# Low one-hots of a PEER gate scatter made by ScalarE, one token at a time

## The reference

```python
q = (x_blk @ w_query).reshape(b, t, PEER_HEADS, 2, HALF_KEY)
scores = jnp.einsum('bthcd,hcnd->bthcn', q, sub_keys)
top_s, top_i = lax.top_k(scores, PEER_TOPK)
...
gate = jax.nn.softmax(best_s, axis=-1)
u = expert_u[expert_idx]
v = expert_v[expert_idx]
act = jax.nn.gelu(jnp.einsum('btd,bthkd->bthk', x_blk, u), approximate=False)
return jnp.einsum('bthk,bthkd->btd', (gate * act), v)
```

## Time and profile before

| | |
|---|---|
| median of 3 runs | 1572.77 us (1571.89 to 1572.81) |
| the profiled execution | 1576.24 us, span 1574.4 us |
| mean granted TensorE clock | 0.928 of full |
| expert scores without gates | about 770 to 977 us |
| gates beside expert scores | 977.7 to 1208.9 us |
| expert values | 1215.2 to 1568.6 us |

### The profile page before, as it was taken

One profiled execution on the slowest core, in us unless ns is written; L12 is line 12 of the kernel. 1 busy time (PEld: TensorE's weight loads), 2 busy tenths in 40 slices (PEclk: granted clock), 3 DMA queues, 4 the chain that ended last, 5 costly groups with the idle time before them and its releaser, 6 DMA issues.

```text
span 1574.4 us, 22797 instructions
## 1 busy us (share of the span) xinstructions
PE 1443.9 (92%) x8952; PEld 1253.7 (80%) x8952; DVE 884.4 (56%) x1571; ACT 745.4 (47%) x1356; POOL 908.5 (58%) x665
## 2 busy tenths in 40 slices
PE   5898998999998599979999989998998999999998
PEld 2685667689886598658999889988998888888886
DVE  4645884356411677543489955999997334322222
ACT  2442212455544466434444445444544555555554
POOL 0540001466765454135679998776776777767775
PEclk9895555999999799989999999999999999999999
DMA  9342342344555132114544545544555666555552
GB/s 387 124 161 107 107 161 107 114 182 163 184 187 187 61 128 108 54 58 149 195 163 163 184 161 182 180 168 168 175 180 204 229 244 249 219 187 189 195 195 90
DMA packets 48298, 261.65 MB, mean 166 GB/s; under 512 B 5440, under 2 KB 14016, under 8 KB 19008
## 3 DMA queue, kind: packets, MB, share of 16 engines
q1 hardware_dynamic: 37984, 249.58, 44.0%
q10 hardware_dynamic: 10208, 10.63, 1.9%
HBM read 250.75 MB, written 9.44 MB: 165 GB/s over the span
## 4 chain that ended last, share of the span: by engine, by line
PE 60%; DVE 24%; PEld 6%; POOL 3%; ACT 3%; issue 2%; DMA 1%; PEldq 1%; DVEq 0%; SPq 0%; ACTq 0%
PE bank L1297 22%; PE bank L699 18%; PE bank L731 17%; PEld bank L731 6%; DVE hotg L2454 5%; DVE hot L2451 4%; DVE hot L2450 4%; POOL v_lo L1782 3%; PE bank L1076 1%; DVE arena L2466 1%; DVE arena L1897 1%; DMA ring<-w_dram 1%; ACT arena L1353 1%; DVE ada L1897 1%; DVE arena L2334 1%
## 5 line engine op out<-in xcount | busy, mean ns | idle before, releaser
L1782 POOL TENSOR_TENSOR v_lo<-ring,v_hi 128x512 fp32r<-128x512 f32 x448 | 614.5, 1386 | 186.3 <-ACT v_hi L1712 176.7
L1774 POOL TENSOR_TENSOR v_lo<-ring,d_hi 128x512 fp32r<-128x512 f32 x213 | 293.7, 1388 | 468.8 <-ACT d_hi L1395 398.8
L1712 ACT CAST v_hi<-ring 128x512 fp32r<-128x512 f32 x512 | 317.3, 621 | 372.4 <-PE bank L699 211.2
L699 PE MATMUL bank<-hT_hi,v_hi 128*128 128x256 f32 x1024 | 294.7, 288 | 9.5 <-POOL v_lo L1782 9.5
L699 PE MATMUL bank<-hT_lo,v_hi 128*128 128x256 f32 x1024 | 289.6, 283 | 0.0
L699 PE MATMUL bank<-hT_hi,v_lo 128*128 128x256 f32 x1024 | 288.1, 281 | 0.0
L1395 ACT CAST d_hi<-ring 128x512 fp32r<-128x512 f32 x236 | 144.0, 620 | 184.9 <-PE bank L731 143.9
L1297 PE MATMUL bank<-v_hi,mix_hi 128*128 128x512 f32 x512 | 202.1, 395 | 3.2 <-DVE mix_lo L2481 3.2
L699 PEld LDWEIGHTS bank<-hT_hi,v_hi 128*128 128x128 f32 x1024 | 194.8, 190 | 11.1 <-POOL v_lo L1782 6.1
L1297 PE MATMUL bank<-v_hi,mix_lo 128*128 128x512 f32 x512 | 200.7, 392 | 0.0
L1297 PE MATMUL bank<-v_lo,mix_hi 128*128 128x512 f32 x512 | 199.2, 389 | 0.0
(11 more groups left out here) (316 smaller groups left out, 2413.0 us busy)
## 6 DMA issues: line engine op xcount, KB each, us to landing
ring<-w_dram SPq DMA_DIRECT2D x228, 1024.0 KB, 4.8
gate_dram<-gput ACTq DMA_DIRECT2D x64, 128.0 KB, 2.4
gget<-gate_dram SPq DMA_DIRECT2D x32, 256.0 KB, 4.9
x<-x_dram SPq DMA_DIRECT2D x1, 1024.0 KB, 5.6
arena<-mem_dram ACTq DMA_DIRECT2D x1, 1024.0 KB, 12.6
out_dram<-x SPq DMA_DIRECT2D x1, 1024.0 KB, 4.0
arena<-const_dram ACTq DMA_DIRECT2D x1, 884.0 KB, 8.7
arena<-vec_dram ACTq DMA_DIRECT2D x1, 144.0 KB, 4.6
```

The costliest lines, as they stand in the source:

```text
L699: return nc.tensor.matmul(out_, lhsT, rhs, start=start, stop=stop)
L1712: nc.scalar.copy(v_hi[:, r, :], quarter(at, r)).then_inc(s_vhi, 1)
L1774: nc.gpsimd.tensor_tensor(v_lo[:, r, :], dense_quarter(d, r), d_hi[:, r, :], ALU.subtract).then_inc(s_dpl, 1)
L1782: nc.gpsimd.tensor_tensor(v_lo[:, r, :], quarter(at, r), v_hi[:, r, :], ALU.subtract).then_inc(s_plo, 1)
```

## The change

`hotg` keeps only the products with the high part of the gates, made by VectorE as before in token pairs. The products with the low part are a new tile `hotl`, two buffers of 4 tokens x 128 keys, with the keys innermost. ScalarE makes it by four activations a group (`Copy` with a scale for each partition), one for each token, which read `hot2` with a step of four. The scale is the low part of the gate in fp32, which now overwrites `gateT`; it is no longer rounded to fp16 ahead of the multiplication. ScalarE does this behind the cast of quarter slot - 2 (and behind `second_gates`, if one stands there), and waits for `hot2` of the group.

```diff
-        hotg = sb("hotg", [2, 2, 2, P, 2], F16)
+        hotg = sb("hotg", [2, 2, P, 2], F16)
+        hotl = sb("hotl", [2, 4, P], F16)
...
                 pe.wait_ge(s_oh, e + 1)
+                pe.wait_ge(s_ohl, e + 1)
                 for i in range(4):
-                    for part in range(2):
-                        last = mm(ps[:, i * P:(i + 1) * P], hot1[:, e % 2, :, i], hotg[:, e % 2, part, i // 2, :, i % 2],
-                                  start=(part == 0), stop=(part == 1))
+                    cols = ps[:, i * P:(i + 1) * P]
+                    mm(cols, hot1[:, e % 2, :, i], hotg[:, e % 2, i // 2, :, i % 2], stop=False)
+                    last = mm(cols, hot1[:, e % 2, :, i], hotl[:, e % 2, i, :], start=False)
...
                     if g in COPY_TURN:
                         second_gates(COPY_TURN[g])
+                    if g + 2 in GATE_TURN:
+                        low_one_hots(GATE_TURN[g + 2])
+
+            def low_one_hots(e):
+
+                if e == 0:
+                    act.wait_ge(s_glo, 1)
+                act.wait_ge(s_eq, e + 1)
+                if e >= 2:
+                    act.wait_ge(s_gfull, e - 1)
+                for i in range(4):
+                    ins = nc.scalar.activation(hotl[:, e % 2, i, :], hot2[:, e % 2, :, i], ACT.Copy,
+                                               scale=gateT[:, 4 * e + i:4 * e + i + 1])
+                ins.then_inc(s_ohl, 1)
...
-            link(tt(gates[:, 1, :], gateT[:, :], gates[:, 0, :], ALU.subtract))
+            tt(gateT[:, :], gateT[:, :], gates[:, 0, :], ALU.subtract).then_inc(s_glo, 1)
...
                 if e >= 2:
                     dve.wait_ge(s_gfull, e - 1)
+                    dve.wait_ge(s_ohl, e - 1)
...
                 dve.wait_ge(s_eq, e + 1)
-                for part in range(2):
-                    ins = tt(hotg[:, b, part], hot2[:, b, :, :].rearrange("p n (a i) -> p a n i", a=2),
-                             gates[:, part, t:t + 4].rearrange("p (a i) -> p a i", a=2).unsqueeze(2).to_broadcast(
-                                 [P, 2, P, 2]), ALU.mult)
-                ins.then_inc(s_oh, 1)
+                tt(hotg[:, b], hot2[:, b, :, :].rearrange("p n (a i) -> p a n i", a=2),
+                   gates[:, 0, t:t + 4].rearrange("p (a i) -> p a i", a=2).unsqueeze(2).to_broadcast([P, 2, P, 2]),
+                   ALU.mult).then_inc(s_oh, 1)
```

More of the change, by code:

```diff
@@ L537, in build @@
         s_oh = sem("onehots_ready")
+        s_ohl = sem("low_onehots_ready")
+        s_glo = sem("low_gates_ready")
         s_gfull = sem("gate_tokens_full")
```

## The result

The changed kernel takes 1590.86 us (median of 4 runs, 1589.23 to 1591.80) against 1572.79: a ratio of 1.0114, 95% interval 1.0096 to 1.0131. It is slower, by 18 us. The forecast was slower by 51: the direction and the place were right, the size wasn't. The profiled execution took 1590.93 us, with a span of 1589.0 (before: 1574.4). The spans differ by 14.6 us and the medians by 18, because the execution profiled before was 3.5 us over its median; what follows goes by the spans.

A forecast was written before the change was run, and what follows sets the result against it. VectorE's throughput was taken to bound the gate stage. The longer lap through ScalarE's order cost 21 us and compares held by GpSimd 30: +51 us, 1624 us for the median, range 1582 to 1650.

The forecast's parts named there:

- What bounds the stage: Gate stage, first to last gate product: VectorE's throughput, slowed by GpSimd's subtractions, sets 3.66 us a lap (one token group).
- the loop: Per lap: hot2, low one-hots, cast, gate copy, gate product, first_gated, next hot2; 3.78 us, 4.0 with extras, 21 us lost.
- VectorE gets 0.33 us a lap back: One of two hotg products leaves VectorE: 20 us over 61 laps, not counted because the lap doesn't wait for it.
- ScalarE's own time: Four added activations a group take 1.2 us; ScalarE then has 3.2 of 3.66 us a lap, so its throughput suffices.
- ScalarE's place: Low one-hots wait for hot2 ahead of the gate copy in ScalarE's order, closing a 4.0 us lap: 21 us lost.
- the way from the end of the copy to TensorE: Semaphore delay between ScalarE's gate copy and TensorE's gate product, taken as 0.14 us from the wait for VectorE.
- a second cast: In 10 of 61 laps a further ScalarE cast of 0.52 us stands in the lap: 0.09 us a lap on average.
- What is late next: GpSimd's subtraction leads VectorE's compare by 0.08 us; lost races cost 1.06 us each, two thirds of 47 laps: 30 us.
- the case I had put at 1635 to 1656: Rival: GpSimd goes ahead of VectorE's compare throughout the gate stage, 1635 to 1656 us; chance 0.17.
- VectorE wins the race: Rival: VectorE's compare goes ahead of GpSimd's subtraction, leaving only the 21 us loss, 1594 us (1580 to 1605); chance 0.26.
- The hidden wait: Rival: ScalarE has room and its wait for hot2 hides; the kernel gets 20 us faster, 1553 us; chance 0.08.
- TensorE's granted clock: Rival: new gaps in the gate stage leave TensorE busy about 72% and lower its clock; no cost taken, no chance given.

The follow-up runs named there:

- the control with the earlier copy: Kernel before the change, with ScalarE's gate copy (second_gates) one quarter earlier: 1568.49 us, ratio 0.9981.
- later: Changed kernel with ScalarE's low one-hots (the hotl activations) one quarter later, at slot - 1: 1562.99 us, ratio 0.9926.
- earlier: Changed kernel with ScalarE's low one-hots one quarter earlier, at slot - 3, in 47 of 64 groups: 1640.79 us, ratio 1.0423.
- Gelu out: Changed kernel with the Gelu put ahead of the low one-hots where these follow a tile's last cast: 1581.73 us, ratio 1.0061.
- copy out: Changed kernel with the gate copy (second_gates) one quarter earlier, at slot + 4, low one-hots unmoved: 1572.91 us, ratio 1.0005.
- the parts alone: Kernel before the change plus only four ScalarE activations without the wait: 1574.31 us; plus only the wait for hot2: 1575.55 us.
- both: Kernel before the change plus the wait for hot2 and four activations on it, written to unread tiles: 1606.55 us, ratio 1.0223.
- the two runs with memsets: Changed kernel with one, or four, 128x1 VectorE memsets ahead of the compare that makes hot2: 1598.78 us and 1630.52 us.

## Why the prediction was right and wrong

**What bounds the stage.** VectorE's throughput, held up by GpSimd's port. Right in the main: with half of its products gone and the loop out of the way, the lap falls to TensorE's 3.37. But the control with the earlier copy gained 3 us on the kernel before without touching VectorE's work, so its throughput wasn't quite all.

**VectorE gets 0.33 us a lap back, and it doesn't count.** Right for the change; VectorE waited 92 us for TensorE. The gain is real only where the loop isn't (1562.99, 1552.92).

**ScalarE's own time.** Four activations: 1.20 forecast, 1.23 measured to the next start, 395 ns each. The Trainium skill ("ScalarE: Activation LUTs", What ACT_TABLE_LOAD costs) gives, by the estimate from its figures, 386 ns and 0.29 apart; here it is 395 and 0.31. That the work fits was right too: alone it left the time at 1.0014.

**ScalarE's place.** Right, and shown from five sides: later (-28 us), earlier (+50), Gelu out (-9), copy out (-18), and the parts alone against both (+2, +3, +34). The loop itself measured 3.64 for a forecast of 3.78. 0.10 of the difference is the way from the end of the copy to TensorE, 0.04 for 0.14: I took the wait for VectorE's `hotg` for it; 0.05 is the compare and its handing over to ScalarE. With that term mended the plain lap is as long as before, and the laps with a Gelu (4.12) and those at the skipped slots carry all of the loss. There I had 0.09 a lap for a second cast, 5 us; measured, the 17 laps at the start and around the skips cost 11.7. The nine held compares are all there, and the eight of them inside the loop lasted 5.4 us longer than unheld ones; how much of the 11.7 is theirs isn't shown.

**What is late next.** This step failed. It gave GpSimd a lead of 0.08 us over the compare and charged two thirds of 47 laps with a lost race, 30 us. Measured, from the start of the cast: the compare 1.96 us (1010.92 to 1012.88, its start in the chain of waits), where I had 2.08, and GpSimd free at 1.96. 35 of the 64 compares began within 0.02 us of GpSimd's subtraction, from 0.02 ahead to 0.01 behind, and VectorE went first in all 35. In 20 others no subtraction was near enough to matter, and 9 were over 0.7 us: those of groups 0, 1, 2 and 4 at the start, and 19, 34 to 36 and 50 behind the skipped slots, all begun while a subtraction was under way. In the regular laps the term was worth 0 and not 30. Its mechanism is there: 0.04 us later and the race is lost, +40 us, which is the case I had put at 1635 to 1656 (it came to 1630.5). The term rests on a lead of 0.08 us, smaller than the error of 0.10 in the way to TensorE alone, so my rows couldn't say which engine was ahead. The rival "VectorE wins the race", 1580 to 1605 at 0.26, is what happened; the range of 1582 to 1650 holds 1590.86 because of this rival, not because of the sum behind the forecast. My working had no ground for the one winner or the other, so that a rival of mine fits is in part luck.

**The other rivals.** The hidden wait is out: ScalarE waited 41 us for `hot` between 980 and 1200 us. TensorE's granted clock stayed at 0.99 in the stage, its upper level (2.4 GHz). It was busy for 221.70 of 248.60 us there, 89%. My 72% for gaps of 1 us in 4 was off in any case: 3 in 4 is 75%.

## What to carry to other kernels

When work moves to another engine, look at what stands behind it in that engine's order and who waits for that; here the same four activations are worth -28 us or +50 by one quarter's place. If a wait closes a loop, add the loop up and compare it with the present lap: two parts, each of them hidden, may not be hidden in sum. Where two engines ask for a port within hundredths of a microsecond, a forecast from delays read to a tenth can't say who wins; take the loss as a range with two ends, and try small shifts on the chip.

## What the runs showed of the hardware

- A compare with two inputs in SBUF that starts just ahead of GpSimd's subtraction runs 0.42 us; some hundredths later it is held until the subtraction ends and lasts 1.56. In the two runs with memsets, the 30 compares from 0.011 us ahead to 0.011 behind the recorded start of the subtraction all ran 0.42, and the 39 that were 0.014 to 0.043 behind all took 1.53 to 1.57. The border isn't the same everywhere: in the kernel before, two operations that began 0.03 us behind a subtraction still ran 0.41.
- Four memsets of 128x1 in a row put off the next VectorE instruction by only 0.04 us, one by 0.01, though each lasts 0.06: they run beside it.
- GpSimd pays when it comes second: in the changed kernel 33 of its 109 subtractions from 980 to 1200 us lasted 1.55 to 1.58 us, each of them begun within 0.02 us of a compare that went first, and no other was over 1.41; most took 1.28. The mean, 1376 ns (1382 before), hides this. VectorE lost 1.1 us when it came second, GpSimd 0.3.
